# A transformer kernel on one core: rotary partners by DMA, norms cut in halves of 256 columns, trunk attentions' weights split piece by piece

## What is computed

```python
y = xf * lax.rsqrt(jnp.mean(xf * xf, axis=-1, keepdims=True) + RMS_EPS)   # rms_norm, times its gain
rot = jnp.concatenate([t1 * cos - t2 * sin, t2 * cos + t1 * sin], axis=-1)  # first block's rotation
def modulate(h, shift, scale):
    return h * (1.0 + scale) + shift
```

## Time and profile before

| | |
|---|---|
| runs | 2554.72, 2556.89, 2557.12 us; median 2556.89 |
| the profiled execution | 2558.64 us, span of its instructions 2556.6 us |
| PE busy | 2482.7 us (97%), weight loads 2088.3 us |
| DVE, ACT, POOL busy | 1308.6, 985.7, 45.2 us |
| granted TensorE clock, mean | 0.992 of full |
| DMA | 356.49 MB, 139 GB/s on average |

### The profile page before, as it was taken

How to read it: one execution, slowest core, us unless ns; L and a number is a source line. 1 busy time by engine, 2 the same in 40 slices (tenths; PEclk the granted TensorE clock), 3 DMA queues, 4 the chain that set the end, 5 groups by cost and what they waited for, 6 DMA issues and landing times.

```text
span 2556.6 us, 39956 instructions
## 1 busy us (share of the span) xinstructions
PE 2482.7 (97%) x16524; PEld 2088.3 (82%) x16524; DVE 1308.6 (51%) x1978; ACT 985.7 (39%) x1482; POOL 45.2 (2%) x71
## 2 busy tenths in 40 slices
PE   8999999999999999999989999999999999989999
PEld 7998899998978888876457888887888887857999
DVE  5478775488753433345663443333433333355654
ACT  5346544366452222252373421224321224355432
POOL 0000000000000000000030000000000000011000
PEclk9999999999999999999999999999999999999999
DMA  6447545454442322334723222234232232633553
GB/s 246 164 149 249 181 165 198 141 182 161 150 167 85 123 83 80 109 116 154 277 102 132 99 92 101 90 112 149 94 112 88 84 122 87 199 141 107 190 191 107
DMA packets 65393, 356.49 MB, mean 139 GB/s; under 512 B 14928, under 2 KB 20176, under 8 KB 29008
## 3 DMA queue, kind: packets, MB, share of 16 engines
q1 hardware_dynamic: 65232, 354.20, 39.5%
HBM read 350.80 MB, written 1.05 MB: 138 GB/s over the span
## 4 chain that ended last, share of the span: by engine, by line
PE 91%; DVE 3%; DMA 2%; ACT 2%; issue 1%; SPq 0%; POOL 0%; DVEq 0%; ACTq 0%; POOLq 0%
PE psum L1269 16%; PE psum L1270 16%; PE psum L1271 16%; PE psum L794 11%; PE psum L831 7%; PE psum L833 6%; PE psum L832 6%; PE psum L906 1%; PE psum L912 1%; PE psum L907 1%; PE psum L1158 1%; DMA wring<-in_w_mod 1%; PE psum L937 1%; PE psum L939 1%; PE psum L938 1%
## 5 line engine op out<-in xcount | busy, mean ns | idle before, releaser
L1269 PE MATMUL psum<-h_hi,w_hi 128*128 128x512 f32 (+1 forms) x1408 | 513.5, 365 | 7.3 <-DVE h_lo L2216 5.9
L1271 PE MATMUL psum<-h_hi,w_lo 128*128 128x512 f32 (+1 forms) x1408 | 511.8, 363 | 0.0
L1270 PE MATMUL psum<-h_lo,w_hi 128*128 128x512 f32 (+1 forms) x1408 | 511.7, 363 | 0.0
L1834 ACT ACTIVATE w_hi<-wring 128x1024 fp32r<-128x1024 f32 (+1 forms) x240 | 273.2, 1143 | 525.8 <-PE psum L1271 518.5
L2392 DVE TENSOR_TENSOR w_lo<-wring,w_hi 128x1024 fp32r<-128x1024 f32 (+1 forms) x240 | 318.6, 1330 | 304.7 <-ACT w_hi L1834 304.3
L831 PE MATMUL psum<-h_hi,w_hi 128*128 128x256 f32 (+1 forms) x1176 | 357.4, 304 | 1.7 <-DVE ring_lo L2247 0.9
L833 PE MATMUL psum<-h_hi,ring_lo 128*128 128x256 f32 (+1 forms) x1176 | 348.7, 297 | 0.0
L832 PE MATMUL psum<-h_lo,w_hi 128*128 128x256 f32 (+1 forms) x1176 | 348.1, 296 | 0.0
L2247 DVE TENSOR_TENSOR ring_lo<-wring,w_hi 128x1024 fp32r<-128x1024 f32 x208 | 246.7, 1222 | 162.9 <-ACT w_hi L1712 161.0
L1269 PEld LDWEIGHTS psum<-h_hi,w_hi 128*128 128x128 f32 x1408 | 266.9, 190 | 52.5 <-issue 7.2
L1271 PEld LDWEIGHTS psum<-h_hi,w_lo 128*128 128x128 f32 x1408 | 266.8, 190 | 41.5
(11 more groups left out here) (202 smaller groups left out, 3319.3 us busy)
## 6 DMA issues: line engine op xcount, KB each, us to landing
wring<-in_w_b_ffn_in SPq DMA_DIRECT2D x80, 1024.0 KB, 4.9
wring<-in_w_mod SPq DMA_DIRECT2D x72, 1024.0 KB, 5.1
wring<-in_w_b_ffn_out SPq DMA_DIRECT2D x64, 704.0 KB, 4.0
wring<-in_w_b_merge SPq DMA_DIRECT2D x24, 1024.0 KB, 4.9
wring<-in_w_b_out SPq DMA_DIRECT2D x16, 1024.0 KB, 5.0
wring<-in_w_b_in SPq DMA_DIRECT2D x16, 1024.0 KB, 6.5
wring<-in_w_b_q SPq DMA_DIRECT2D x12, 1024.0 KB, 4.9
wring<-in_w_b_k SPq DMA_DIRECT2D x12, 1024.0 KB, 4.8
```

What stands on the lines that cost most here:

```text
L1269: nc.tensor.matmul(acc, wh[:, k, :], rhs_hi[k], start=(k == 0), stop=False)
L1270: nc.tensor.matmul(acc, wh[:, k, :], rhs_lo[k], start=False, stop=False)
L1271: return nc.tensor.matmul(acc, wl[:, k, :], rhs_hi[k], start=False, stop=(k == n - 1))
L1834: A(part_piece(w_hi, q, i), raw_piece(c, i), ACT.Copy).then_inc(weights_rounded, 1)
```

## The change

The diff has these parts.

1. **Rotation of the first block.** The 16 products with `rot_half` for branches 0 and 1 are gone. SP copies for each tile the partner rows (8 partitions x 512, four copies of 8 rows) into a buffer `partner` (two tiles), right behind the DMA of the chunk four places on, waiting for ACT's copy of the tile and for the rotation of the tile two before. DVE computes the rotation from SBUF alone (`rope_tile`), three instructions of the same size as before. The index query and key are still rotated by PE.
2. **Norms.** The sums, roots, reciprocals and spreads are made per half of 256 columns (64 columns each in four groups). ACT writes `h_hi` directly from the modulation and the plain value in a second pass; for tile 0 DVE computes the plain value. `first_passes` puts the two passes with `h_hi` of the first four steps ahead of their `h_lo` passes. Modulation chunks are cut in halves of four products and stand at places given by `CHAIN`; what is left is issued inside the first pieces (`late_mods`).
3. **Weight order.** In `b2.0.nm` and `b2.1.nm` both of the mixer's first chunks come after two modulation chunks (before: one after three, one after four); in `b2.1.n1` the feed-forward's second chunk comes after three of five.
4. **Trunk attentions.** A step's weight chunk is rounded and split in single pieces, in four steps in place of two, on DVE behind the reciprocals; in `b2.1.att` the modulation chunks stand in steps 1, 2, 4, 5, 7 (before 2 to 5), one more than before and one fewer in `b2.1.heads`; the convolution's norm and gates stand one to four steps earlier, its root is taken straight from PSUM; in both, T(t-2) stands ahead of the modulation on PE. ACT loads the exponential's table ahead of the attention (`early_exponential`).
5. The last feed-forward and mixer additions to x are signalled per 256 columns.

```diff
-              ("b2.0.heads", 6), ("b2.0.att", 7), ("b2.0.n2", 3), ("b2.1.n1", 5), ("b2.1.nm", 4), ("b2.1.heads", 6), ("b2.1.att", 4),
+              ("b2.0.heads", 6), ("b2.0.att", 7), ("b2.0.n2", 3), ("b2.1.n1", 5), ("b2.1.nm", 4), ("b2.1.heads", 5), ("b2.1.att", 5),
...
+def first_passes(N):
+    order = FIRST_SHORT if N == SEQ else FIRST
+    head = order[0:4]
+    return [(k, i, 0) for k, i in head] + [(k, i, 1) for k, i in head] + [(k, i, part) for k, i in order[4:] for part in range(2)]
+CHAIN = {"b2.0.n1": (1, 0, 2, 0, 3), "b1.1": (1, 0, 1, 0, 2), "b2.1.n2": (1, 0, 1, 0, 2), "b2.0.nm": (1, 1, 1, 1, 0), "b2.1.nm": (1, 1, 1, 1, 0)}
...
-        for at, c in ((6, 0), (8, 1)):
-            out[at].append(("split", 0, c))
+        for piece, at in enumerate((5, 6, 7, 8)):
+            out[at].append(("part", 0, piece))
...
+                if c in ROTARY_AT:
+                    if E.new(copied_label):
+                        sp.wait_ge(*E.at(copied_label))
...
+                    for b in (0, 8, HD, HD + 8):
+                        other = b + 8 if b % HD == 0 else b - 8
+                        sp.dma_start(partner[b:b + 8, m % 2, :], view[other:other + 8, :]).then_inc(s_partner[m % 2], 16)
...
+                norm_mods(chain[0])
+                for h in range(halves):
+                    last_sums(nm, h)
+                    norm_mods(chain[1 + h] if halves == 2 else chain[2])
+                for h in range(halves):
+                    if E.new(f"{nm}.root.{h}"):
+                        pe.wait_ge(*E.at(f"{nm}.root.{h}"))
+                    spread_half(f"{nm}.rs.{h}", banks[h], rs, h, SEQ // GROUPS * h)
+                    norm_mods(chain[3 + h] if halves == 2 else chain[4])
...
-                        if kind == "mod":
+                        if kind == "mod" and nm[1] == "1":
                             modulation(l, c)
...
+                    for kind, l, c in fill[t]:
+                        if kind == "mod" and nm[1] == "2":
+                            modulation(l, c)
                     if t >= 3:
...
+                def rope_tile(m):
+                    dve.wait_ge(s_partner[m % 2], 64 * (4 * l + m // 2 + 1))
+                    V.tensor_tensor(partner[:, m % 2, :], partner[:, m % 2, :], C("sin_part"), ALU.mult).then_inc(roped, 1)
+                    V.tensor_tensor(view, view, C("cos_part"), ALU.mult).then_inc(roped, 1)
+                    V.tensor_tensor(view, view, partner[:, m % 2, :], ALU.add).then_inc(roped, 1)
```

More of the change, by code:

```diff
@@ L119, in fillers @@
     if nm == "b2.1.att":
-        for at, c in ((6, 0), (8, 1)):
-            out[at].append(("split", 1, c))
+        for piece, at in enumerate((4, 5, 7, 8)):
+            out[at].append(("part", 1, piece))
     return out
@@ L983, in norm, with spread_half @@
+            def spread_half(label, bank, roots, h, at):
+                acc = take(label, fixed=bank)
+                per = SEQ // GROUPS
+                for j in range(GROUPS):
+                    row = C("ident")[:, GW * j:GW * j + 1].broadcast_to([P, P])
+                    mm = product(acc[:, SEQ * h + per * j:SEQ * h + per * j + per], row, rs[:, at:at + per], 0, 1)
+                mm.then_inc(summed, 1)
+                E.step(summed, label)
             def norm(nm, summed_before=0):
-                per = NORM_N[nm] // GROUPS
@@ L994, in norm @@
-                acc = take(f"{nm}.rs", fixed=(bank + 5) % BANKS)
-                if E.new(f"{nm}.root"):
-                    pe.wait_ge(*E.at(f"{nm}.root"))
-                for j in range(GROUPS):
-                    row = C("ident")[:, GW * j:GW * j + 1].broadcast_to([P, P])
-                    mm = product(acc[:, per * j:per * j + per], row, rs[:, 0:per], 0, 1)
-                mm.then_inc(summed, 1)
-                E.step(summed, f"{nm}.rs")
-                norm_mods(nm, middle, None)
+                state["rows_bank"], *banks = norm_banks(nm, [book.banks[f"{nm}.sum.{h}"] for h in range(halves)])
@@ L1004, in hold @@
             def hold(nm):
+                state["todo"] = [(m, a) for m in MODS.get(nm, []) for a in range(2)]
                 if nm == "b1.1":
@@ L1064, in joint_norm @@
+                norm_mods(chain[0])
                 joint_sums(range(KD - 1, KD))
-                norm_mods(nm, early, middle)
-                acc = take(f"{nm}.rs", fixed=(q0 + 5) % BANKS)
+                if E.new("context.root"):
+                    pe.wait_ge(*E.at("context.root"))
+                spread_half(f"{nm}.rs.1", banks[1], rs, 1, SEQ // GROUPS)
+                norm_mods(chain[2])
                 if E.new("joint.root"):
                     pe.wait_ge(*E.at("joint.root"))
-                for j in range(GROUPS):
-                    row = C("ident")[:, GW * j:GW * j + 1].broadcast_to([P, P])
-                    mm = product(acc[:, P * j:P * j + P], row, rs[:, 0:P], 0, 1)
@@ L1233, in modulation @@
                 per = KD // GROUPS
-                for a in range(per):
+                for a in some:
                     for j in range(GROUPS):
@@ L2176, in joint_norm @@
                     ahead(i)
+                per = SEQ // GROUPS
+                if E.new("context.sum'"):
+                    dve.wait_ge(*E.at("context.sum'"))
+                V.reciprocal(rs[:, per:2 * per], rs[:, per:2 * per]).then_inc(normed, 1)
+                E.step(normed, "context.root")
                 if E.new("joint.c7"):
```

439 lines of the change are left out of this document (269 added, 170 removed).

## The result

The changed kernel takes 2566.61 us (median of 6 runs, 2563.79 to 2569.49), the kernel before, beside it, 2557.01. The ratio is 1.0039, 95% interval 1.0028 to 1.0050: 10 us slower, where 36 us faster was forecast. The profiled execution has a span of 2565.6 us against 2556.6 us, so it shows the loss: 9.0 us.

What follows compares the result with a forecast made beforehand. PE was taken to bound the kernel, busy 2482.7 of 2556.6 us. Terms 13.8 + 6.5 + 8.5 + 3.5 + 3.4 = 35.7 us off the median 2556.89 gave 2521.2 us, range 2513 to 2530.

Steps and rivals of the forecast that it cites:

- rotations: First block's projections: 16 rotations of 0.86 us leave PE, with the partner copies hidden; 13.8 us off.
- part 2: Norms: half-wise sums and direct h_hi start first passes sooner, most given back at the third piece's split; 6.5 us off.
- both chunks now come early: b2.0.nm: the mixer's first two chunks arrive early, so waits for modulation weights and the second chunk's split shrink; -1.2 us.
- Part 3: b2.1.heads and b2.1.att: waits for modulation, first exponentials, table load and transposes shrink; 1.54 + 1.0 + 1.28 + 4.7 = 8.5 us off.
- single pieces stand behind the reciprocals: b2.1.att, steps 6 and 8: splits no longer precede the reciprocals, so 4.7 of 5.2 us of PE waits go.
- Its time is free there: b2.1: the moved modulation chunk (1.0 us) fills PE's 2.25 us wait for the first exponentials before step 2's scores.
- table load term: b2.1.att: the exponential's table load moves ahead of the attention into ACT's idle time; 1.28 us off.
- Part 4: b2.0.att: waits from table loads, DVE's splits and gates and the end shrink, less 2 us new waits; 3.5 us off.
- Part 5: Clock: the 6.82 us window at 1.2 GHz at 2142.90, behind a modulation wait, goes; 3.4 us off.
- leave the other four: Clock: of five listed windows at 1.2 GHz, 27.32 us together, four were assumed to stay.
- Only the removed work counts: Rival, chance 0.17: new waits replace old ones in norms and attentions; 13.8 + 0 + 4 + 0.5 = 18 off, 2538.6 us.
- The copies hold SP: Rival, chance 0.03: first block's partner copies make SP issue next weights late; at 3 us per set, 12 slower, 2569 us.

Runs made afterwards that it cites:

- three: Changed kernel with bias copies one chunk earlier, three modulation chunks before the mixer's first two, and b2.1.att's output-weight pieces a step later; 2539.85 us, ratio 0.9930.
- three_rot: `three` with the first block's sixteen rotations back on PE, no partner copies on SP and DVE's sums at their former places; 2554.08 us, ratio 0.9987.
- bias_early: Changed kernel with the 32 bias copies issued on SP behind the sixth chunk of b2.1.in instead of the seventh; 2555.17 us, ratio 0.9989.
- order: Changed kernel with three modulation chunks, not two, ahead of the mixer's first two chunks in b2.0.nm and b2.1.nm; 2553.67 us, ratio 0.9986.
- best: `three` with convolution gates one per step (7 to 10), b2.1.att's modulation chunks in steps 1, 2, 6, 7, 8 and pieces in 6 to 9; 2538.40 us, ratio 0.9923.

## Why the prediction was wrong

Its sum was 35.7 us off; the profile shows 9.0 us on top, 44.7 us apart. Term by term, the clock's share where it fell counted in:

| term | forecast | in the profile |
|---|---|---|
| rotations (both layers' projections) | -13.8 | -15.9, of it -1.7 clock |
| eight norms, with the clock's -3.4 | -9.9 | -1.3 |
| b2.1.heads and att | -8.5 | -0.6 |
| b2.0.att | -3.5 | +0.1 |
| third chunk, twice (in the trace against `three`) | none | +12.7 |
| seventh chunk behind the biases | none | +12.2 |
| b1.0.att (in this profile; 0.6 at most in the others but `three_rot`) | none | +3.2 |

The remaining -1.4 us are the convolution and the latent projections; PE's wait for the convolution's copies fell there from 1.1 to 0.3. In b1.0.att PE waits 2.2 us for an exponential at 204.12, where the kernel before waits 0.6 and `three` 0.4, and a slow window of 3.4 us stands behind it; why in this execution, no run shows.

- **The direction failed in part 2, "both chunks now come early".** I looked at the two chunks that were moved and not at those behind them in a ring of four. Whoever takes a slot early keeps it from the fourth after it: 12.7 us. My own rule, to name what is queued behind, I applied to SP's new copies alone.
- **The biases were in no term.** The change moves 32 DMAs of SP by one chunk without a line of the diff on them, since their place is counted within a run of chunks: 12.2 us, 10.0 of them the wait and some 2.4 clock. Either of these two mended alone turns the sign, if only just (`bias_early` 0.9989, `order` 0.9986). SP's whole list in both orders, not the three places that the diff led me to, would have shown the copies one chunk further down.
- **Part 3 (b2.1) failed at "single pieces stand behind the reciprocals".** The pieces do stand there, and the waits for POOL in `b2.1.att` did shrink. But the first piece was put where its weights had not landed (2.4 us), and with that mended PE waits for ACT's exponentials and copies instead: in `three`, from 2240 to 2305 us,

```profile
PE psum L1224 <- ACT slab L1892: 3.1, 3, 1.4
PE psum L1224 <- POOL slab L2239: 3.0, 9, 1.3
PE psum L1224 <- ACT slab L1867: 1.4, 2, 1.2
```

  A step with a piece costs ACT 1.06 + 2 x 0.88 + 2 x 0.6 = 4.0 us, and PE's step without modulation is 3.1. I priced the waits by who ended them, not by the next engine's full step. The wait for modulation in b2.1.heads stayed (1.5 us before, 1.7 after): one chunk fewer did not make the others land sooner. "Its time is free there" failed too. PE's waits of the changed kernel from 2218 to 2275 us:

```profile
PE psum L831 <- DMA wring<-in_w_mod: 1.7, 1, 1.7
PE psum L950 <- DVE ring_lo L2397: 1.5, 1, 1.5
PE psum L1221 <- ACT slab L1864: 1.4, 2, 1.2
```

  The second was 0.4 before. DVE's split of the last chunk of `b2.1.in` stands behind nine instructions of the heads' rotation, and the modulation chunk that was moved away had filled PE's time up to it: of its 1.0 us nothing is won in heads. In the attention the wait of 2.25 us for the first exponentials is gone, but the transposes of step 2, now ahead of the chunk, wait 1.4 for them. The table load term, 1.28, is right.
- **Part 4** failed in the same manner. Behind exponentials PE waits 3.7 us in `three` where the earlier trace rows had 1.7, and at the end behind POOL 2.0 of 3.2.
- **Part 2's sizes.** b2.0.n2 gave 0.9 of the 1.0 forecast, and by the steps given: its first pass starts 2.2 us sooner (2.7 forecast), its third step 0.9, behind the split of the third piece. (DVE's steps listed there add up from +5.3 to +11.0; the +11.5 has half a microsecond for ACT's pass that no row gave.) b1.1's norm gained nothing, with a slow window in it (the change) or without one (`order`). The joint norm itself, from 716 us of the kernel before on, lost 1.8 us with 10.2 us of slow window in it and gained 1.0 in `order`, where there is none (the table's stage also holds a slow window at 658 us that the kernel before alone has there). b2.1.nm's own gain and window came to 1.5 against 3.8: where the rest of the window's 3.4 went is not shown; PE may have waited there for the next hurdle anyway. b2.1.n2, forecast at -0.8, lost 1.6. PE waits 2.0 us for the reciprocal there (1.6 before) and 1.3 for late tiles' `h_lo` (0.9 before); the waits account for some 0.8 of it, and the rest was not taken apart.

```profile
PE psum L831 <- DVE rs L2263: 2.0, 1, 2.0
PE psum L1379 <- DVE h_lo L2363: 1.3, 2, 0.7
```

- **Part 5.** The window at 2142.90 went and one at 2163.41 came. The earlier trace rows has five windows of 27.32 us, but the profile before has nine, 44 us in all; "leave the other four" left out the rest. The signs that I listed as wrong (PE waiting for `h_lo` of late tiles, slow windows moved, not gone) are what is seen.
- **The rivals.** "Only the removed work counts", 2538.6, is near what is left when the three waits are mended: `three` takes 2539.85. Its terms are met less well than its sum (2.8 us in b2.1.heads and att, 1.7 of them clock, where it had 4, and none in b2.0.att, where it had 0.5), so the closeness is partly luck. "The copies hold SP" had the right engine and sign with the wrong copies: 16 sets of partner rows cost PE nothing, 32 bias copies already in the program cost 12 us. Its chance of 0.03 came of looking at new instructions only.

## What to carry to other kernels

When weights come through a ring from one list, a chunk that is moved forward takes a slot from the one that stands a ring's length behind: walk the whole list, and for every chunk write down when its slot comes free and when it is needed. Compare the full DMA queue in both orders, for transfers whose place is computed may move with no line changed; and for each, ask who stands waiting for it with what behind. A gain read from a wait is only as large as the distance to the next engine's full step. And a filler moved out of one place uncovers the wait that it filled there: price both places.

## What the runs showed of the hardware

- Small copies hold the issuing queue by number, not size: 32 of 64 KB took SP 22.53 us, 0.70 each, four partner copies of 8 rows 2.64 to 2.90 in the rows above, while a 1 MB chunk takes 0.33 to 0.44 as a rule and 0.65 right behind the bias copies. The Trainium skill ("DMA: Bandwidth & Descriptors", Rules for kernel authors) says that spreading DMAs over several engines' queues saves only issue time. Issue time is what was short here; that remedy was not tried.
- A slow window doesn't follow from PE's waits alone. One of 10.24 us lay in the joint norm of the changed kernel with PE busy all through, behind waits of 0.8 and 1.6 us. `bias_early` and `order` reach this norm at the same time (the waits end at 708.1 us in both) and have the same two waits: `bias_early` has such a window from 707.35 on, `order` has none. What decides between them no run here shows.
- I take the clock for the largest source of scatter: the six runs of `best` lie between 2530.1 us, at a mean clock of 0.996, and 2540.8, with 0.991 to 0.993 in the three slowest; over the 22 runs of the kernel before beside the first experiments, time and mean clock have a correlation of -0.84.
